# Both halves of the first modulation summed on VectorE, small loads spread over three queues

## The reference

```python
mod = silu(c) @ w_ada + b_ada            # c: (1, 2048), w_ada: (2048, 12288)
sh_a, sc_a, gt_a, sh_f, sc_f, gt_f = split(mod, 6)
h = rmsnorm(x, g_pre_attn) * (1 + sc_a) + sh_a      # x: (256, 2048)
proj = h @ w_in                                     # w_in: (2048, 6144)
...
mem_n = rmsnorm(mem, g_mem)                         # mem: (256, 2048)
k, v = mem_n @ w_k_cross, mem_n @ w_v_cross         # (2048, 512) each
```

## Time and profile before

| | before |
|---|---|
| median of three executions | 2635.37 us |
| the profiled execution | 2638.07 us |
| its span, first to last instruction | 2636.7 us |
| TensorE busy | 2491.6 us, 94% |
| VectorE busy | 1614.3 us, 61% |
| ScalarE busy | 1164.6 us, 44% |
| GpSimd busy | 31.0 us, 1% |
| mean granted clock of TensorE | 0.968 of full speed |
| moved by the loads and stores | 530.55 MB, 201 GB/s over the span |

### The profile page before, as it was taken

One profiled execution on the slowest core, in us unless ns is written; L12 is line 12 of the kernel. 1 busy time (PEld: TensorE's weight loads), 2 busy tenths in 40 slices (PEclk: granted clock), 3 DMA queues, 4 the chain that ended last, 5 costly groups with the idle time before them and its releaser, 6 DMA issues.

```text
span 2636.7 us, 28981 instructions
## 1 busy us (share of the span) xinstructions
PE 2491.6 (94%) x11623; PEld 2081.0 (79%) x11623; DVE 1614.3 (61%) x1751; ACT 1164.6 (44%) x1449; POOL 31.0 (1%) x62
## 2 busy tenths in 40 slices
PE   5999998798999999999998999898799999999998
PEld 5888777577888888878886888777688888788886
DVE  5558988798886757555545575455454444455555
ACT  3324454345443444444445444545444444444443
POOL 0000000100000000000000000000000000000000
PEclk9999999798999999999998999999899999999999
DMA  7889867296786566655664656144266666555553
GB/s 269 300 302 345 292 228 244 95 341 225 279 296 223 180 188 190 191 169 192 193 190 132 198 160 193 39 166 153 75 190 185 187 185 185 177 196 193 194 194 116
DMA packets 221235, 530.55 MB, mean 201 GB/s; under 512 B 17462, under 2 KB 20780, under 8 KB 220460
## 3 DMA queue, kind: packets, MB, share of 16 engines
q1 hardware_dynamic: 218240, 526.58, 61.0%
q10 hardware_dynamic: 2860, 2.11, 0.3%
HBM read 526.53 MB, written 2.10 MB: 200 GB/s over the span
## 4 chain that ended last, share of the span: by engine, by line
PE 89%; DVE 7%; ACT 2%; issue 1%; DMA 1%; ACTq 1%; POOL 0%; DVEq 0%
PE ps L493 27%; PE ps L495 27%; PE ps L494 27%; PE ps L489 2%; PE ps L546 2%; DVE silu_gate L1640 1%; DVE ada_acc L1283 1%; PE ps L618 1%; PE ps L595 1%; PE ps L563 1%; DVE neg_max L1412 1%; DVE wlo L1269 1%; DVE w_s L1411 1%; DMA chunk<-in_k_chunk 1%; PE ps L607 0%
## 5 line engine op out<-in xcount | busy, mean ns | idle before, releaser
L907 ACT ACTIVATE whi<-raw 128x1024 fp32r<-128x1024 f32 (+1 forms) x802 | 848.2, 1058 | 1279.9 <-PE ps L495 1193.4
L1269 DVE TENSOR_TENSOR wlo<-raw,whi 128x1024 fp32r<-128x1024 f32 (+1 forms) x802 | 974.3, 1220 | 563.3 <-ACT whi L907 561.9
L493 PE MATMUL ps<-whi,h_hi 128*128 128x512 f32 (+1 forms) x1952 | 771.7, 395 | 3.5 <-DVE wlo L1269 2.5
L495 PE MATMUL ps<-wlo,h_hi 128*128 128x512 f32 (+1 forms) x1952 | 763.0, 391 | 0.0
L494 PE MATMUL ps<-whi,h_lo 128*128 128x512 f32 (+1 forms) x1952 | 762.8, 391 | 0.0
L493 PE MATMUL ps<-whi,src_hi 128*128 128x512 f32 x1152 | 452.8, 393 | 11.7 <-DVE src_lo L1363 7.5
L494 PE MATMUL ps<-whi,src_lo 128*128 128x512 f32 x1152 | 452.2, 393 | 0.0
L495 PE MATMUL ps<-wlo,src_hi 128*128 128x512 f32 x1152 | 451.9, 392 | 0.0
L493 PEld LDWEIGHTS ps<-whi,h_hi 128*128 128x128 f32 x1952 | 369.4, 189 | 81.1 <-DVE wlo L1269 4.8
L495 PEld LDWEIGHTS ps<-wlo,h_hi 128*128 128x128 f32 x1952 | 369.1, 189 | 77.2
L494 PEld LDWEIGHTS ps<-whi,h_lo 128*128 128x128 f32 x1952 | 369.3, 189 | 74.0 <-issue 0.5
(11 more groups left out here) (241 smaller groups left out, 1374.4 us busy)
## 6 DMA issues: line engine op xcount, KB each, us to landing
raw<-in_w_up SPq DMA_DIRECT2D x216, 512.0 KB, 3.8
raw<-in_w_down SPq DMA_DIRECT2D x216, 512.0 KB, 3.9
raw<-in_w_ada SPq DMA_DIRECT2D x192, 512.0 KB, 5.8
raw<-in_w_in SPq DMA_DIRECT2D x168, 512.0 KB, 4.5
raw<-in_w_gate SPq DMA_DIRECT2D x88, 512.0 KB, 3.9
raw<-in_w_out SPq DMA_DIRECT2D x64, 512.0 KB, 4.6
raw<-in_w_k_cross SPq DMA_DIRECT2D x8, 512.0 KB, 5.7
raw<-in_w_v_cross SPq DMA_DIRECT2D x8, 512.0 KB, 5.3
```

Source lines behind the costliest of these rows:

```text
L493: T.matmul(dst, ah, bh, start=first, stop=False)
L495: return T.matmul(dst, ah, bl, start=False, stop=last)
L907: A.activation(whi[n % SPLIT][:, 0:size], raw[f % RAW][:, 0:size], ACT.Copy).then_inc(*s_hi.next(n))
L1269: V.tensor_tensor(wlo[n % SPLIT][:, 0:size], raw[w_fetch[n] % RAW][:, 0:size], r32(whi[n % SPLIT][:, 0:size]), ALU.subtract).then_inc(*s_l ...
```

## The change

- The first 64 tiles of w_ada are now 128 rows x (512 shift columns and the 512 scale columns of the same quarter), 16 tiles for a quarter. They are of the same size as before and are loaded in nearly the same turns.
- All of them go through VectorE's `ada_block`, one operation over 1024 columns for each tile, into `acc[kt % 2]`. `ada_products`, its semaphore `s_gv` and the reduction in `first_gain` are gone. `ada_block_sums` sums 8 blocks of 128 columns for a quarter instead of 4.
- mem's transposes go to eight different banks, all 32 in a row.
- Small loads: c and the unit matrix are issued by SyncE ahead of mem and x; frequencies, positions, lambda's rows and the two masks by GpSimd ahead of its roots; ScalarE keeps the 11 loads of parameter rows. Lambda's rows and the masks get a semaphore of their own, `s_parl`.
- x's rows are scaled on ScalarE, behind mem's copies.
- In `h_group` for the first norm `norm_f` is made by ScalarE behind each pair of `h_hi`; VectorE keeps one subtraction for each pair.
- VectorE takes one of the first six tiles after each of the first six pairs of mem's low parts, and the first two weight tiles after the fourth and the sixth.

```diff
-    ADA = [(part, p // 8, p % 8) for p in range(32) for part in (1, 0)]
+    ADA = [(None, c, kt) for c in range(4) for kt in range(KD)]
...
-    for p in range(3, 32):
-        ada_at[p - 3 if p < 17 else 14 + (p - 17) * 6 // 5] += [2 * p, 2 * p + 1]
+    for i in range(6, 64):
+        ada_at[(i - 6) // 2 if i < 34 else 14 + (i - 34) * 17 // 30].append(i)
...
     def sync_program(Y):
+        Y.dma_start(vec1[0:16, :], a["c"].rearrange("o (k n) -> (o k) n", n=P)).then_inc(*s_parc.next())
+        Y.dma_start(ident[:, :], a["k_ident"]).then_inc(*s_parc.next())
         Y.dma_start(memt[:, :, :], a["mem_2"][0].rearrange("(m p) d -> p m d", p=P)).then_inc(*s_mem.next())
...
-                part, c, q = ADA[i]
-                src = a["w_ada"][0][2 * q * P:(2 * q + 2) * P, part * D + c * BANK:part * D + (c + 1) * BANK].rearrange("(k p) n -> p k n", p=P)
-                dst = raw[r][:, :].rearrange("p (k n) -> p k n", k=2)
+                _, c, kt = ADA[i]
+                src = a["w_ada"][0][kt * P:(kt + 1) * P, 0:2 * D].rearrange("p (t n) -> p t n", t=2)[:, :, c * BANK:(c + 1) * BANK]
+                dst = raw[r][:, :].rearrange("p (t n) -> p t n", t=2)
...
     def pool_program(G):
...
+        G.dma_start(inv[:, :], a["k_inv"].to_broadcast([P, NROT])).then_inc(*s_park.next())
+        for i, name in enumerate(("positions", "positions_2")):
+            for m in range(MT):
+                G.dma_start(posi[:, 2 * i + m:2 * i + m + 1], a[name].rearrange("o (m p) -> m p o", p=P)[m]).then_inc(*s_park.next())
+        for i, name in enumerate(("lambda_q1", "lambda_k1", "lambda_q2", "lambda_k2")):
+            G.dma_start(lamv[:, i, :], a[name].to_broadcast([P, 64])).then_inc(*s_parl.next())
+        G.dma_start(causal[:, :], a["k_causal"]).then_inc(*s_parl.next())
+        G.dma_start(chunk[:, :], a["k_chunk"]).then_inc(*s_parl.next())
         G.wait_ge(*s_half.at())
...
         def ada_block_sums(c):
             T.wait_ge(*s_ada.at(16 * c + 15))
-            for b in range(4):
-                col = ps[:, 6 + c % 2, 64 + b:65 + b]
-                c_b = slice(c * BANK + b * P, c * BANK + (b + 1) * P)
+            for b in range(8):
+                col = ps[:, 6 + c % 2, b:b + 1]
+                c_b = slice((c % 2) * TILE + b * P, (c % 2) * TILE + (b + 1) * P)
...
             if n + 2 in IN_READY:
-                ada_block_sums(IN_READY.index(n + 2))
+                c = IN_READY.index(n + 2)
+                T.wait_ge(*(s_gsc.at("in", c - 2) if c > 1 else s_meml.at(7)))
+                ada_block_sums(c)
...
+                for kt in (k, k + 1):
+                    if kt >= 8:
+                        A.wait_ge(*s_hl.at(i, (kt - 8) // 2))
+                    ins = A.activation(norm_f[:, kt % 8, :], xT[:, kt, :], ACT.Identity, scale=gain[:, kt:kt + 1], bias=shift[:, kt:kt + 1])
                 ins.then_inc(*s_hh.next(i, k // 2))
...
+        for m in range(MT):
+            A.wait_ge(*s_rsq.at("x", m))
+            A.activation(norm_x[m][:, :], x[:, m, :], ACT.Copy, scale=sq2[:, m:m + 1]).then_inc(*s_nxa.next("x", m))
         A.wait_ge(*s_lam.at())
...
         def ada_block(i):
...
+            dst, src, w = acc[kt % 2][:, (c % 2) * TILE:(c % 2 + 1) * TILE], raw[f % RAW][:, :], sil[:, kt:kt + 1]
+            if kt < 2:
+                if c > 1:
+                    V.wait_ge(*s_adat.at("in", c - 2))
+                V.tensor_scalar(dst, src, w, None, ALU.mult).then_inc(*s_ada.next(i))
+            else:
+                V.wait_ge(*s_ada.at(i - 2))
+                V.scalar_tensor_tensor(dst, src, w, dst, ALU.mult, ALU.add).then_inc(*s_ada.next(i))
...
             ins.then_inc(*s_meml.next(b))
-            if b % 3 == 1:
-                ada_block(ADA_FIRST[2 * (b // 3) + 1])
-            if b % 3 == 2:
-                low(b // 3)
+            if b < 6:
+                ada_block(ADA_FIRST[b])
+            if b in (3, 5):
+                low(b // 2 - 1)
```

More of the change, by code:

```diff
@@ L323, in build @@
     s_raw = [signal(f"s_raw{r}", 16) for r in range(RAW)]
[L324 to L326 removed]
+    s_parc, s_park, s_parl, s_par, s_mem, s_x, s_late, s_gfin, s_out = (signal(n, 16) for n in ("s_par_c", "s_par_k", "s_par_l", "s_par", "s_mem", "s_x", "s_late", "s_gfin", "s_out"))
+    s_hi, s_lo, s_mm, s_ada = (signal(n) for n in ("s_hi", "s_lo", "s_mm", "s_ada"))
     s_srch, s_srcl = signal("s_src_hi"), signal("s_src_lo")
@@ L643, in tensor_program @@
         for g in range(4):
[L644 to L652, removed]
+            transposes(2 * g, [(k * S + m * P, memt[:, m, (4 * g + k) * P:(4 * g + k + 1) * P])
+                               for k in range(4) for m in range(MT)]).then_inc(*s_memt.next(g))
+        T.wait_ge(*s_one.at())
         for n in range(40):
@@ L927, in h_group @@
                         ins = A.activation(h_hi[:, kt, :], src, ACT.Identity, scale=gain[:, kt:kt + 1], bias=shift[:, kt:kt + 1])
+                if i != H_IN:
+                    ins.then_inc(*s_hh.next(i, k // 2))
+                    continue
+                for kt in (k, k + 1):
+                    if kt >= 8:
+                        A.wait_ge(*s_hl.at(i, (kt - 8) // 2))
+                    ins = A.activation(norm_f[:, kt % 8, :], xT[:, kt, :], ACT.Identity, scale=gain[:, kt:kt + 1], bias=shift[:, kt:kt + 1])
                 ins.then_inc(*s_hh.next(i, k // 2))
@@ L992, in unit_step @@
                     A.activation(u["out"](t), pair_of(u, t)[:, 0, 0:2 * P].rearrange("p (h n) -> p h n", h=2), ACT.Copy).then_inc(*s_oa.next(name, t))
[L995 to L1000, removed]
         A.wait_ge(*s_vec2.at())
@@ L1030, in scalar_program @@
                 kt = 2 * b + kk
-                ins = A.activation(mem_hi[:, kt, :], ps[:, MEM_BANKS[b], kk * S:(kk + 1) * S], ACT.Copy, scale=cols[:, C_GMEM + kt:C_GMEM + kt + 1])
+                ins = A.activation(mem_hi[:, kt, :], ps[:, b, kk * S:(kk + 1) * S], ACT.Copy, scale=cols[:, C_GMEM + kt:C_GMEM + kt + 1])
             ins.then_inc(*s_memh.next(b))
@@ L1285, in ada_block @@
         def ada_block(i):
-            part, c, q = ADA[i]
+            _, c, kt = ADA[i]
             f = ada_fetch[i]
             V.wait_ge(*s_raw[f % RAW].at(f))
-            for kk in range(2):
-                dst, src = acc[kk][:, c * BANK:(c + 1) * BANK], raw[f % RAW][:, kk * BANK:(kk + 1) * BANK]
-                w = sil[:, 2 * q + kk:2 * q + kk + 1]
-                if q == 0:
-                    ins = V.tensor_scalar(dst, src, w, None, ALU.mult)
-                else:
-                    if kk == 0:
-                        V.wait_ge(*s_ada.at(i - 2))
-                    ins = V.scalar_tensor_tensor(dst, src, w, dst, ALU.mult, ALU.add)
-            ins.then_inc(*s_ada.next(i))
+            dst, src, w = acc[kt % 2][:, (c % 2) * TILE:(c % 2 + 1) * TILE], raw[f % RAW][:, :], sil[:, kt:kt + 1]
[6 more added lines that the diff above has]
+                V.scalar_tensor_tensor(dst, src, w, dst, ALU.mult, ALU.add).then_inc(*s_ada.next(i))
         def beat(n):
@@ L1304, in beat @@
                     ada(i)
-                elif i % 2:
+                else:
                     ada_block(i)
@@ L1345, in h_group @@
                         ins = V.scalar_tensor_tensor(h_lo[:, kt, :], src, gain_[:, kt:kt + 1], r32(h_hi[:, kt, :]), ALU.mult, ALU.subtract)
+                elif i == H_IN:
+                    ins = V.tensor_tensor(h_lo[:, k:k + 2, :], norm_f[:, k % 8:k % 8 + 2, :], r32(h_hi[:, k:k + 2, :]), ALU.subtract)
                 else:
@@ L1514, in vector_program @@
         V.tensor_scalar(lam[:, 3:4], lam[:, 2:3], -(0.8 - 0.6), None, ALU.add)
-        for m in range(MT):
-            V.wait_ge(*s_rsq.at("x", m))
-            V.tensor_scalar(norm_x[m][:, :], x[:, m, :], sq2[:, m:m + 1], None, ALU.mult).then_inc(*s_nx.next("x", m))
         for n in range(40):
```

36 lines of the change are left out of this document (6 added, 30 removed).

## The result

| | before | after |
|---|---|---|
| median, the executions beside each other | 2633.49 us (2627.82 to 2638.07) | 2606.14 us (2603.63 to 2608.98) |
| ratio, 95% interval | | 0.9897 [0.9873, 0.9922] |
| the profiled execution; its span | 2638.07; 2636.7 us | 2608.47; 2607.1 us |
| TensorE, VectorE, ScalarE, GpSimd busy | 2491.6, 1614.3, 1164.6, 31.0 us | 2449.4, 1633.7, 1176.1, 37.0 us |
| mean granted clock of TensorE | 0.968 | 0.965 |

The change gained 27.35 us by the medians (1.0%), 11 less than the 38 forecast. The time lies inside the stated range (2584 to 2617) but 1 us above the forecast's own one (2588 to 2605), and it is nearer to rival A's 2609 than to the 2597 forecast, although A did not come: the time alone would have spoken for the wrong mechanism. The first stage ended 13 us later than forecast.

A forecast was written before the change was run, and what follows sets the result against it. TensorE was taken to bound the first stage. Afterwards start 26.0, 134 to the last scale tile and 28 behind it end it at 188, not 228.8: 41 less, taken as 38, giving 2597 us; own range 2588 to 2605, stated 2584 to 2617.

The forecast's parts named there:

- rival A: Start: GpSimd's queue is late, positions land at 27.2; gain only 27 us, 2609; chance 0.12.
- The start, T = 26.0: T is the start of mem's transposes on TensorE: forecast at 26.0 us, 4.9 earlier, with positions landing at 15.7.
- T to the first tile, 11.2: From the start of mem's transposes to TensorE's first weight tile: 11.2 us, against 13.7 before.
- T + 134: Last scale tile of the first stage, 134 us after mem's transposes start, at 160 us.
- rival B: First stage: loads don't reach 385 GB/s but stay at 330; gain 20 us, 2615; chance 0.13.
- step (5): x's rows and norm_f move to ScalarE: hidden, except at the last h group, where h_lo comes 1 us later.
- the 3 us for VectorE and loads waiting for one another: First stage: loads alone end at T + 131, VectorE alone at T + 127; mutual waits make it T + 134.
- The tail, 28 less the 1.2: Behind the last scale tile: VectorE's operation and sums 5, two tiles 5.4, h_lo 1.1, tiles 34 to 39 16.3; together 28 us.
- costs half of its 6.8 us: A half-clock stretch in the stage's last 28 us costs half of 6.8 us; the gain of 41 is taken as 38.
- Rival C, half clock throughout: First stage: TensorE stays at 1.2 GHz as it waits before each tile; 38 us slower, 2673; chance 0.03.
- The copy near 188: Sign of being right: ScalarE's copy behind tile 39, the first stage's end, near 188 us instead of 228.8.
- TensorE waits about 1 us before each tile: Sign of being right: from 60 to 160 us TensorE waits about 1 us per tile for VectorE's low part.

The follow-up runs named there:

- Experiment 1: Changed kernel with ScalarE making a quarter's row blocks of h ahead of the high part of weight tile n + 3; 2596.9 us, 0.9872 of the kernel before.
- experiment 5: Changed kernel with ScalarE's h group first, sums one tile later, and one accumulator (16 summing products a quarter, not 32); 2588.9 us, 0.9850 of the kernel before.
- experiment 3: Changed kernel with ScalarE's h group first and TensorE's sums of a quarter one weight tile later; 2593.5 us, 0.9854 of the kernel before.
- experiment 2: Changed kernel with only TensorE's sums of a quarter moved one weight tile later; 2599.2 us, 0.9880 of the kernel before.
- experiment 10: Changed kernel with ScalarE's h group first and one accumulator (16 sums a quarter), sums in their old place; 2591.7 us, 0.9851 of the kernel before.
- experiment 11: The version of experiment 5 with norm_f made by VectorE again; 2590.0 us, 0.9840 of the kernel before.
- experiment 4: Changed kernel with a product of 504 columns, result dropped, behind each pair of summing products; 2613.7 us, 0.9938 of the kernel before.

## Why the prediction was right, and where it was off

The mechanism holds: with the products gone (no L546 in the page), the loads and VectorE pace the stage, and the whole gain is in it. By the steps of the sum:

- **The start, T = 26.0:** measured 23.33, 2.7 earlier. The chain from the positions on was right (10.3 us forecast, 9.9 measured; for the upper end the prediction adds 10.1 where its own terms give 10.3); the positions landed at 13.4 and not at 15.7, a term that it had taken between two ends and had no row for. VectorE, which it calls idle until 17.63, had a few short operations before (0.8 us), which changes nothing. Rival A did not come.
- **T to the first tile, 11.2:** measured 11.2.
- **T to the fourth quarter's sums.** The sum has T + 134 for the last scale tile and 1.2 for its operation, T + 135.2; they began at 168.18 = T + 144.9, 9.7 late. The rate was right: 386 to 390 GB/s where the queue was full, as in the earlier trace rows, so rival B did not come. What failed is step (5), "ScalarE is busy 6.2 of 20 us, so they are hidden except at the last h group", and with it the 3 us for VectorE and loads waiting for one another. Busy share was the wrong view: ScalarE had time, but its h groups stood behind a wait for TensorE, and VectorE and the load queue behind them, at the ends of the quarters before the last too. Experiment 1 changes this alone and brings the sums to 159.53 = T + 136.4, 1.2 from the forecast.
- **The tail, 28 less the 1.2:** from the first sum to the stage end 26.8 forecast, 33.0 measured. The sums took 6.25 us for 3.8 and tiles 32 and 33 took 7.9 for 5.4, both because of the half clock: 4.9 us, where "costs half of its 6.8 us" had set 3.4 aside. The wait for h_lo was as forecast (1.16 for 1.1), and from tile 34 to the last copy it took 17.7 for 16.3. In experiment 1 the tail is 28.3.
- **Together:** -2.7 + 9.7 + 6.2 = +13.2, which is 201.2 for 188; 3.4 of it was in the forecast already, as the step from 41 to 38. From T to the stage end the sum said 162; experiment 1 takes 164.7 and experiment 5, with half of the sums, 161.8.
- **Rival C, half clock throughout:** the granted clock over 60 to 156 us is 0.86, not 0.5, and the kernel is not slower. But its seed was there: 7 to 10 us at 0.50 at each quarter's end, from within the sums on. I had taken 264-288, where VectorE paces TensorE at a clock of 1.00, as the model for the whole stage; it has no such place. The Trainium skill, "TensorE: Matmul & The Clock Gate", section "HAM oscillation", has a kernel whose waits for loads, 3 to 5 us each, between groups of wide products bring the half clock back. The trace of experiment 5 agrees in this, with waits of 2.07 to 3.69 us at the start of its three stretches, though TensorE waited there for ScalarE's copies and a low part and not for a load itself. The waits of about 1 us that the prediction expected are shorter than that page's, so the page spoke less for rival C than the prediction made it. In experiment 3 the clock falls with no wait ahead of the sums, so waits are not the only thing that it falls with here.
- **What was to show it:** VectorE over 80% held (77.65 of 96 us, 81%), no L546, a granted clock above 0.8 from 60 to 156 and later stages as long as before. The copy near 188 came at 201, for the reasons above. Two more signs failed. The loads made 353 GB/s over 60 to 156 and not above 370; in experiment 1 they made 387. And "TensorE waits about 1 us before each tile" is not there: it was idle 7.2 us of 96, and 5.6 of these are the two waits ahead of the sums, at 96.09 and 132.17. The half clock used up part of its slack; how much, no run shows.

When the clock falls can be read from these traces, though each kernel has only one. In experiments 2 and 3 rows of 32 one-column products with no wait ahead, and in experiment 10 rows of 16 behind waits of 2.2 to 3.4 us, have half clock at all four places; in experiments 5 and 11 rows of 16 with no wait have it at none of eight. In 5 and 11 all six stretches begin in a wait of 2.1 to 3.7 us between tiles or at most 1.4 us behind it. In the kernel before the sums of three quarters stand directly behind a block of 16 of L546, 32 in a row, and two of the three have it; at the fourth the sums stand alone, at full clock. So the half clock goes with the summing products in some places and with TensorE's waits in others. What it is in the products that does it, and why wide products among them don't shorten it (experiment 4), stays open. No run takes the sums away altogether. Nor was the changed kernel run beside experiment 1 on one chip.

## What to carry to other kernels

Before work is called hidden on an engine that is idle half the time, look at what stands ahead of it in that engine's own order: here 4 us of work behind a wait of 9 us for a buffer held VectorE for 6.4 us, TensorE for 1.2 and the load queue for 8. When a stage's bound moves from one engine to the loads, order each engine's turn so that whatever the others wait for comes ahead of whatever waits for a free buffer. And here a clock that halves was cheap while the loads paced the stage (experiment 1: 24.0 us of it at 387 GB/s); it cost in the tail, 4.9 us, and through the waits that it lengthened.

## What the runs showed of the hardware

- Two of the trace's one-column products take 0.22 us from start to start at full clock and 0.43 at half. 32 in a row went with 7 to 10 us at a granted clock of 0.50 at each of four places in the changed kernel, with 3 to 10 us in experiments 1 to 3, and with 10 to 14 us with eight products of 504 columns among them (experiment 4). 16 in a row with no wait ahead ran at full clock at all eight places of experiments 5 and 11.
- In experiments 5 and 11 all six stretches of half clock behind 56 us, 3 to 7 us long, began in a wait of TensorE of 2.1 to 3.7 us between tiles of wide products, or at most 1.4 us behind it. One wait of 2.03 us, up to 59.72 in experiment 5, had no half clock in the 20 us behind it.
- Eleven small loads on GpSimd's queue took some 0.53 us each to issue, from 1.30 to 7.3 us, and landed after 7.0 (76 KB), 8.2 (the positions) and up to 12.8 us (128 KB), while SyncE's queue brought mem and x. The positions were there 4.2 us earlier than from ScalarE's queue.
- The load queue held 386 to 387 GB/s over 96 us in loads of 0.524 MB, two of three of them in pieces of 2 KB, a partition's 512 shift and 512 scale columns (experiments 1, 3, 5 and 10).
